# Feed-forward networks of a two-block transformer kernel: gate and up products with stationary tokens and 512 streamed columns

## What is computed

```python
def swiglu(h, w_gate_up, w_down):
    gu = jnp.einsum("bsd,df->bsf", h, w_gate_up)
    g, u = jnp.split(gu, 2, axis=-1)
    return jnp.einsum("bsf,fd->bsd", jax.nn.silu(g) * u, w_down)

h = rmsnorm(x, norm_ffn_pre[l])      # first block; x = x + rmsnorm(f, ...)
x = x + 0.5 * swiglu_2(rms_norm(x, norm_ffn1), w1, w3, w2)   # second block, twice
```

## Time and profile before

| | |
|---|---|
| runs | 1048.45, 1049.71, 1050.58 us; median 1049.71 |
| span of the profiled execution | 1046.5 us |
| its time against the median | the span is from first to last instruction; 3.2 us below the median of the runs |
| instructions in it | 19409 |
| mean granted TensorE clock | 0.994 of full |
| chain that ended last | TensorE 88% of the span, DVE 7%, issue 2%, ACT, POOL and DMA 1% each |
| mean DMA rate | 168 GB/s |

### The profile page before, as it was taken

One profiled execution on the slowest core, in us unless ns is written; L12 is line 12 of the kernel. 1 busy time (PEld: TensorE's weight loads), 2 busy tenths in 40 slices (PEclk: granted clock), 3 DMA queues, 4 the chain that ended last, 5 costly groups with the idle time before them and its releaser, 6 DMA issues.

```text
span 1046.5 us, 19409 instructions
## 1 busy us (share of the span) xinstructions
PE 1022.3 (98%) x8282; PEld 1007.0 (96%) x8282; DVE 651.0 (62%) x616; ACT 493.6 (47%) x625; POOL 115.3 (11%) x91
## 2 busy tenths in 40 slices
PE   8999999998999999989999999999999999999997
PEld 7998999998999999979999999999999999999996
DVE  6655767958655555595555557775684475555554
ACT  5443445645433434554343434655755564343433
POOL 5000000566000000450000002000030020000000
PEclk9999999999999999999999999999999999999999
DMA  8653364453545565545646464633444345555531
GB/s 277 206 163 120 121 242 162 134 188 122 200 162 200 164 198 168 182 137 198 197 164 200 160 200 162 200 123 122 162 161 147 116 161 168 194 171 190 183 138 41
DMA packets 138107, 175.39 MB, mean 168 GB/s; under 512 B 3940, under 2 KB 122950, under 8 KB 137926
## 3 DMA queue, kind: packets, MB, share of 16 engines
q1 hardware_dynamic: 136006, 171.24, 49.7%
q10 hardware_dynamic: 2048, 3.38, 0.9%
HBM read 173.56 MB, written 1.05 MB: 167 GB/s over the span
## 4 chain that ended last, share of the span: by engine, by line
PE 88%; DVE 7%; issue 2%; ACT 1%; POOL 1%; DMA 1%; SPq 0%; DVEq 0%; ACTq 0%; POOLq 0%
PE bank L373 27%; PE bank L374 27%; PE bank L375 27%; DVE act_lo L1437 3%; DVE w_lo L1424 1%; PE bank L457 1%; DVE x_T L1539 1%; PE bank L821 1%; PE bank L842 1%; DMA stage<-in_w_in 1%; ACT w_hi L899 1%; PE bank L460 0%; PE bank L600 0%; DVE w_lo L1561 0%; PE bank L616 0%
## 5 line engine op out<-in xcount | busy, mean ns | idle before, releaser
L373 PE MATMUL bank<-act_hi,w_hi 128*128 128x256 f32 x1648 | 471.8, 286 | 12.7 <-DVE act_lo L1437 9.2
L374 PE MATMUL bank<-act_lo,w_hi 128*128 128x256 f32 x1648 | 467.5, 284 | 0.0
L375 PE MATMUL bank<-act_hi,w_lo 128*128 128x256 f32 x1648 | 467.4, 284 | 0.0
L373 PEld LDWEIGHTS bank<-act_hi,w_hi 128*128 128x128 f32 x1648 | 317.3, 193 | 18.1 <-DVE act_lo L1437 7.6
L374 PEld LDWEIGHTS bank<-act_lo,w_hi 128*128 128x128 f32 x1648 | 317.6, 193 | 0.1
L375 PEld LDWEIGHTS bank<-act_hi,w_lo 128*128 128x128 f32 x1648 | 317.4, 193 | 0.0
L1430 DVE TENSOR_TENSOR w_lo<-stage,w_hi 128x2048 fp32r<-128x2048 f32 x81 | 185.6, 2292 | 141.3 <-ACT w_hi L906 141.3
L1424 DVE TENSOR_TENSOR w_lo<-stage,w_hi 128x2048 fp32r<-128x2048 f32 x79 | 183.9, 2333 | 90.1 <-ACT w_hi L899 89.7
L899 ACT ACTIVATE w_hi<-stage 128x2048 fp32r<-128x2048 f32 x79 | 150.7, 1910 | 72.9 <-PE bank L375 71.0
L906 ACT ACTIVATE w_hi<-stage 128x2048 fp32r<-128x2048 f32 x81 | 154.0, 1902 | 54.8 <-PE bank L375 54.8
L373 PE MATMUL bank<-ffn_hi,w_hi 128*128 128x256 f32 x480 | 135.9, 283 | 0.0
(11 more groups left out here) (300 smaller groups left out, 1233.9 us busy)
## 6 DMA issues: line engine op xcount, KB each, us to landing
stage<-in_ffn_w SPq DMA_DIRECT2D x66, 1024.0 KB, 5.1
stage<-in_w_in SPq DMA_DIRECT2D x33, 1024.0 KB, 5.2
stage<-in_w_gate_up SPq DMA_DIRECT2D x22, 1024.0 KB, 5.1
stage<-in_w_down SPq DMA_DIRECT2D x11, 1024.0 KB, 4.8
stage<-in_w_out SPq DMA_DIRECT2D x8, 1024.0 KB, 4.9
stage<-in_mem_w_kv SPq DMA_DIRECT2D x8, 1024.0 KB, 5.3
stage<-in_w_branch SPq DMA_DIRECT2D x4, 1024.0 KB, 5.4
stage<-in_mem_w_q SPq DMA_DIRECT2D x4, 1024.0 KB, 4.9
```

The costliest lines, as they stand in the source:

```text
L373: pe.matmul(dst, w, x, start=first, stop=False, skip_group_check=not group)
L374: pe.matmul(dst, w, lo_x, start=False, stop=False, skip_group_check=not group)
L375: return pe.matmul(dst, lo_w, x, start=False, stop=last, skip_group_check=not group)
```

## The change

A gate or up chunk becomes half of the features (512) of 256 gate columns and the same 256 up columns, side by side, so a chunk pair covers the same weights. The tokens are stationary and 512 columns are streamed: 2 token halves by 4 feature blocks by 3, 24 matmuls a chunk; bank 0 holds token half 0 (256 gate columns, then 256 up columns), bank 1 token half 1. The factor of the norm is per partition now: two numbers per partition (`tok`), from sums by token, which ACT's silu and DVE's product take as a scale. The hidden values come out with tokens on partitions; TensorE turns them back with four transposes a pair into bank 3, from which ACT and DVE make the high and low parts. Each gate/up chunk is loaded by two DMAs of 512 KB. The order in the loop is first half, transposes, second half, down. Before its first chunk a network waits until both banks have been read.

```diff
+            def gate_up(c, half, w_g, g_col, w_u, u_col, place):
+                free(c)
+                to = stage[:, place, :].rearrange("p (k s n) -> p k s n", k=KD // 2, s=2)
+                ks = slice(half * KD // 2, (half + 1) * KD // 2)
+                for i, (w, col) in enumerate(((w_g, g_col), (w_u, u_col))):
+                    sp.dma_start(to[:, :, i, :], w.rearrange("(k p) n -> p k n", p=P)[:, ks, bass.ds(col, 2 * P)]
+                                 ).then_inc(landed[place], 16)
...
-            def down(c, place, hid_hi, hid_lo, first, done=None, cleared=None):
+            def down(c, place, hid_hi, hid_lo, first, done=None, cleared=None, between=None):
                 for m in range(KD):
+                    if between is not None and m == KD // 2:
+                        between()
...
+            def gate_up(place, half, ready=None, base=0, freed=None):
+                wh = w_hi[:, place, :].rearrange("p (k n) -> p k n", k=KD // 2)
+                wl = w_lo[:, place, :].rearrange("p (k n) -> p k n", k=KD // 2)
+                for t in range(2):
+                    if freed is not None:
+                        pe.wait_ge(hid_done, freed + t + 1)
+                    ts = slice(t * P, t * P + P)
+                    for i in range(KD // 2):
+                        k = half * KD // 2 + i
+                        if ready is not None and t == 0:
+                            pe.wait_ge(ready, base + k + 1)
+                        mm = three(bank[UP + t][:, :], act_hi[:, k, ts], act_lo[:, k, ts], wh[:, i, :], wl[:, i, :],
+                                   k == 0, k == KD - 1)
+                    if half and t == 0:
+                        mm.then_inc(gate_up_half, 1)
+                mm.then_inc(used, 1)
...
+                def turn_hidden(i):
+                    pe.wait_ge(hid_done, i * 2 + (2 * PAIRS * f + 2))
+                    for m in range(2):
+                        for t in range(2):
+                            mm = pe.transpose(pair[AUX][:, m, t * P:t * P + P], h_tok[:, t, m * P:m * P + P], ident)
+                    mm.then_inc(hid_turned, 1)
...
+                for c in before:
+                    wait_read(pe, c)
+                pe.wait_ge(lo_done, base + 1)
+                gate_up(base % RING, 0, act_lo_done, 8 * prep)
+                sums_by_token(norm)
+                pe.wait_ge(lo_done, base + 2)
+                gate_up((base + 1) % RING, 1, act_lo_done, 8 * prep)
+
+                def body(t, first=False, between=None):
                     c = base + 2 + t * 3
                     pe.wait_ge(lo_done, c + 1)
+                    gate_up(s[0], 0, freed=t * 2 + 2 * PAIRS * f)
                     if first:
                         aux(A_BEFORE_FFN[f])
+                    turn_hidden(t)
                     if first and extra is not None:
                         extra()
+                    pe.wait_ge(lo_done, c + 2)
+                    gate_up(s[1], 1)
+                    ffn_down(c + 2, t, s[2], first, between=between)
+                body(PAIRS - 2, between=lambda: turn_hidden(PAIRS - 1))
+                ffn_down(last, PAIRS - 1, last % RING, last=True)
...
-            feed_forward(1, 3, 5)
+            feed_forward(1, 3, 5, (MEMV[1], MEMV[2]))
+            pe.wait_ge(hid_done, 4 * PAIRS)
...
+            def token_deviation(n):
+                act.wait_ge(sum_done, n + 1)
+                act.wait_ge(rs_done, made(n - 1))
+                act.activation(tok_std, bank[SUM][:, 0:2], ACT.Sqrt, bias=eps, scale=1.0 / D).then_inc(std_done, 1)
...
+                def hidden(t, i, chunk):
+                    for q in range(2):
+                        if q:
+                            act.wait_ge(used, t * 3 + (chunk + 1))
+                        else:
+                            act.wait_ge(gate_up_half, t + (f * PAIRS + i + 1))
+                        act.activation(silu[:, q, :], bank[UP + q][:, 0:2 * P], ACT.Silu, scale=tok[:, q:q + 1]
+                                       ).then_inc(silu_done, 1)
                 def hidden_hi(t, i, after, to):
-                    act.wait_ge(h_done, t + (f * PAIRS + i + 1))
+                    act.wait_ge(hid_turned, t + (f * PAIRS + i + 1))
                     if after is not None:
                         act.wait_ge(used, after)
-                    act.activation(to, h_T, copy).then_inc(ffn_hi_done, 1)
+                    act.activation(to, pair[AUX], copy).then_inc(ffn_hi_done, 1)
+                def body(t, after):
                     hi_in_loop(t, base + 4)
+                    hidden_hi(t, 0, after, ffn_hi[:, :, :])
                     hi_in_loop(t, base + 5)
+                    hidden(t, 1, base + 3)
                     hi_in_loop(t, base + 6)
...
+                def hidden(t, i):
+                    for q in range(2):
+                        dve.wait_ge(silu_done, t * 2 + (2 * (f * PAIRS + i) + q + 1))
+                        dve.scalar_tensor_tensor(h_tok[:, q, :], bank[UP + q][:, 2 * P:4 * P], tok[:, q:q + 1], silu[:, q, :],
+                                                 ALU.mult, ALU.mult).then_inc(hid_done, 1)
+                def hidden_lo(t, i, to=ffn_lo[:, :, :], of=ffn_hi[:, :, :]):
+                    dve.wait_ge(ffn_hi_done, t + (f * PAIRS + i + 1))
+                    dve.tensor_tensor(to, pair[AUX], of.bitcast(F32), ALU.subtract).then_inc(ffn_lo_done, 1)
+                def body(t):
+                    lo_in_loop(t, base + 4)
+                    hidden_lo(t, 0)
+                    lo_in_loop(t, base + 5)
+                    hidden(t, 1)
+                    lo_in_loop(t, base + 6)
...
-            factor(5, rs)
+            token_factor(5)
```

More of the change, by code:

```diff
@@ L40, with is_gate_up, landings @@
 FFN_CHUNKS = 3 * PAIRS
-def ffn_ups(base):
-    inner = [base + 2 + 3 * t + i for t in range(PAIRS - 2) for i in (0, 2)]
-    return [base, base + 1, *inner, base + FFN_CHUNKS - 4, base + FFN_CHUNKS - 3]
+def is_gate_up(c):
+    return any(b <= c < b + FFN_CHUNKS - 1 and (c - b < 2 or (c - b - 2) % 3 < 2) for b in FFN)
+def landings(c):
+    return 16 * sum(2 if is_gate_up(x) else 1 for x in range(c % RING, c + 1, RING))
 BANK, BEFORE, FREED = {}, {}, {}
@@ L161, in build @@
         m_T = gate[:, 8:16, :]
-        g_s, silu, u_s, h_T = (gate[:, 2 * i:2 * i + 2, :] for i in range(4))
+        silu, h_tok = gate[:, 2:4, :], gate[:, 6:8, :]
         sel = table[:, 0:4, :].rearrange("p a b -> p (a b)").rearrange("p (h m) -> p h m", h=8)
@@ new lines, in feed_forward, with ffn_down @@
+            def feed_forward(f, prep, norm, before, extra=None):
+                base = FFN[f]
+                s = [(base + 2 + j) % RING for j in range(3)]
+                def turn_hidden(i):
[4 more added lines that the diff above has]
+                    mm.then_inc(hid_turned, 1)
+                def ffn_down(c, i, place, first=False, last=False, between=None):
+                    pe.wait_ge(ffn_lo_done, i + (f * PAIRS + 1))
+                    hid_hi, hid_lo = (act_hi, act_lo) if last else (ffn_hi, ffn_lo)
+                    down(c, place, hid_hi, hid_lo, first, down_done if last else None,
+                         k_done if f == 0 and first else None, between)
+                for c in before:
[6 more added lines that the diff above has]
+                def body(t, first=False, between=None):
@@ L508, in body @@
[L508 to L512, removed]
+                    pe.wait_ge(lo_done, c + 2)
+                    gate_up(s[1], 1)
+                    ffn_down(c + 2, t, s[2], first, between=between)
+                body(0, True)
                 with pe.Fori(1, PAIRS - 2) as t:
-                    body(t, "")
+                    body(t)
@@ L975, in exps, with feed_forward @@
                 e.then_inc(exp_done, 1)
[L977 to L983, removed]
+            def feed_forward(f, norm):
+                base = FFN[f]
+                def hidden(t, i, chunk):
[6 more added lines that the diff above has]
+                                       ).then_inc(silu_done, 1)
@@ L1000, in feed_forward @@
+                with act.Fori(1, PAIRS - 2) as t:
+                    body(t, t * 3 + (base + 2))
                 last = base + FFN_CHUNKS - 1
                 hi(last - 1)
-                hidden(PAIRS - 2, 1)
+                hidden_hi(PAIRS - 2, 0, last - 3, ffn_hi[:, :, :])
                 hi(last)
-                hidden_hi(PAIRS - 2, 1, last - 1, act_hi[:, 0:2, :])
+                hidden(PAIRS - 2, 1, base + 3)
+                hidden_hi(PAIRS - 1, 0, last - 1, act_hi[:, 0:2, :])
                 if last + 1 < CHUNKS:
@@ L1445, in factor, with token_factor @@
                 dve.wait_ge(rs_done, made(n))
+            def token_factor(n):
+                dve.wait_ge(std_done, n + 1)
+                dve.reciprocal(tok[:, :], tok_std).then_inc(rs_done, 1)
+                dve.wait_ge(rs_done, made(n))
             def result(c):
@@ L1517, in feed_forward @@
-                body(0, pair[AUX])
```

(8 more changed lines are left out.)

103 lines of the change are left out of this document (30 added, 73 removed).

## The result

The changed kernel is **slower**, by 0.9%: 1059.34 us (median of 4 runs) against 1049.62 for the kernel before (4 runs), a ratio of 1.0094, 95% interval 1.0079 to 1.0110. The forecast was 1040.6, with a range from 1034 to 1059.

What follows compares the result with a forecast made beforehand. Bound by the rate at which TensorE takes instructions: 21.9 us gained in the steady part, less 5.9, 4.0 and 2.9, is 9.1 off the 1046.5 us span; with 3.2 for the median, 1040.6 us, range 1034 to 1059.

Steps and rivals of the forecast that it cites:

- The price of 512 columns: Gate/up matmuls: 512 float32r columns start 0.216 us apart, bounds 0.213 to 0.240, the weight load hidden behind the longer stream.
- Rival 1: Every gate/up matmul: fixed part paid per instruction, 0.227 us each, 1057 us, chance 0.15; nothing saved, 0.240, 1077, chance 0.06.
- The start of the first two networks: Waiting for ACT's reads of both banks puts the second chunk off by 5.9 us in the first, 4.0 in the second.
- the clock: First chunk of the first two networks: TensorE at 1.2 GHz after idling, about 1.6 us lost in each.
- The start of the third: Third network: no loss, second chunk waits for DVE's low part as now; a possible 1.6 us clock fall taken as none.
- The stall behind the first pair: First two networks: the second pair's first half waits for the first pair's products, 1.45 us each, 2.9 in all.
- The transposes: Four for each of 11 pairs per network, 0.109 us each, 4.8 us a network.
- rival 3: Transposes in each pair cost their record's length, 0.272 us instead of 0.109: 21.5 us more, 1062 us, chance 0.03.
- The loop's waits and the loads: Inside the loop: ACT and DVE finish ahead of TensorE, banks free 4.6 us ahead; halved loads cost nothing.
- rival 4: A new wait in each pair, on DVE or the subtraction: 0.5 us a pair gives 16 us, 1057 us, chance 0.06.
- The median against the span: Whole run: the median lies 3.2 us above the profiled span of 1046.5 us, and the same difference was taken for the forecast.
- Rival 2: Networks' starts cost less, as the clock stays up or reads come sooner, with half the stalls: 1036 us, chance 0.13.

Runs made afterwards that it cites:

- experiment 9: A kernel of nothing but matmuls, in blocks by data type and column count; float32r took 0.230 us for 512 columns, 0.118 for 256.
- experiment 5: The kernel before, with only the wait for the reads of both banks ahead of a network's first chunk added: 1061.58 us, ratio 1.0106.
- experiment 6: The changed kernel with TensorE's idle time at the networks' starts filled by unused float32 matmuls, the waits left: 1055.29 us, ratio 1.0057 to the kernel before.
- experiment 4: The changed kernel without the 132 transposes, down products multiplying untransposed hidden values: 1045.28 us, ratio 0.9962 to the kernel before.
- 1: The changed kernel, waiting for each bank only ahead of the token half that goes there: 1053.12 us, ratio 1.0031 to the kernel before.
- 2: The changed kernel with waits by bank and ACT's reads of the last key and value banks moved forward: 1048.57 us, ratio 0.9993 to the kernel before.
- 7: The changed kernel with waits by bank, ACT's reads moved forward and short fillings of unused matmuls at the networks' starts: 1046.50 us, ratio 0.9971 to the kernel before.

## Why the prediction was wrong

- **The price of 512 columns: this step failed.** I took 0.216 us from the float32 rows and gave 0.227, "the fixed part is paid per instruction", 0.15. It measured 0.227: 1512 x 0.011 = 17 us, most of the 23 us between the forecast and the span. Rival 1 gave 1057 and was the right mechanism; that it came within 2.4 us of the measured median is in part luck. Its span would have been 1054.0, 6.1 below the measured 1060.1, and 4.0 of that is hidden by the step to the median: 3.2 us were added, where the changed kernel's profiled execution lies 0.8 above its median. The argument that misled me was the row at 1.2 GHz: 256 columns at 213 ns, "no further cost shows". That is true, and 512 columns at 0.427 at 1.2 GHz confirm it; but it says nothing of the full clock, where the fixed part does show. 64 columns take the same 0.213 at 1.2 GHz (experiment 9), so this row could not weigh streaming against the load at all. The float32 rows were of another data type: experiment 9 shows that float32 and bf16 have a small fixed part, 0.002 to 0.003, and float32r the large one, and 0.120 for 256 float32r columns had it in plain sight.
- **The start of the first two networks: right, a little short.** 5.9 and 4.0 forecast, 6.6 and 5.2 measured; experiment 5 shows the wait alone to cost 11.8. The mis-sized term is the clock (1.6 us each, where experiment 6 took 2.1 and 2.6 away) and the dearer first chunk (0.3 each).
- **The start of the third: right**; the low clock that I put at nothing came in the profiled execution and cost some 1.6 us behind it.
- **The stall behind the first pair: right**, 1.16 us instead of 1.45 (0.227 to 1.39 between two starts).
- **The transposes: right**, 14.4 forecast, 14.1 by experiment 4; rival 3 is out.
- **The loop's waits and the loads: right.** No wait of TensorE on DVE or ACT inside the loop; rival 4 is out.
- **The median against the span: mis-sized.** I added 3.2 us to the forecast span for what lies around a span; but the profiled execution of the kernel before was the fastest of its runs, and a run's own time is only 1.8 us above its span. The changed kernel's profiled execution was its slowest instead, so 13.7 us in the spans are 9.7 in the medians.

Rival 2 assumed cheaper starts. They did not come by themselves, but could be repaired: 1048.6 with the reads early, level with the kernel before, and 1045.7, 0.4% faster, with the clock kept up. Its 1036 assumed 0.216 a matmul, and no version came near it.

## What to carry to other kernels

Streaming more columns per matmul saved a fixed cost per instruction here, not a share of the time: take that cost from the same data type (distance between starts minus columns by clock), multiply by the matmuls that go, and set it against what the new layout adds. When a buffer's use is widened (both banks instead of one), look up who frees it and what stands ahead of that read in its queue: here reads of about 1 us, behind six to eight other instructions, cost 11.8 us, more than twice the 4.8 that was left of the longer streams after the transposes (18.9 - 14.1). Waiting by bank and moving the reads made the changed kernel 10.8 us faster.

## What the runs showed of the hardware

- A float32r matmul cost its columns at 2.4 GHz and 0.012 to 0.017 us more, for 256 to 512 streamed columns and 128 stationary ones, and 0.009 to 0.018 more with 32 and 64 stationary ones; bf16 0.002 to 0.003 more; at 1.2 GHz float32r 512 columns took 0.427, nothing more.
- Below 256 columns float32r kept a floor: 0.110 for 128 columns and 0.112 for 64 at 2.4 GHz, 0.213 for 64 at 1.2 GHz.
- Filling gaps with unused matmuls kept the granted clock at 2.4 GHz and made the kernel faster, 4.1 us in experiment 6, with the waits left as they were. Whether a gap brought the clock down differed between executions: 1.88 us in the third network was followed by a fall in the changed kernel and experiment 4, not in 1 and 2; 2.14 us near 218, the same code in all, was followed by one in the kernel before, not in experiments 5 and 7. Once the clock fell without any gap, in the block of 64 columns of experiment 9.
